# Mask products between the attention units of a two-block transformer kernel, and compressed-attention products at other steps

## The reference, cut to what matters

```
p_cmp = masked_softmax(q @ kc.T, valid_c)      # compressed keys: one per 16 tokens, 32 columns kept
o_cmp = p_cmp @ vc                             # kc, vc: a two-layer gelu MLP over blocks of 32 tokens
o_slc = masked_softmax(q @ ks.T, causal) @ vs  # all blocks are selected at 512 tokens
o_win = masked_softmax(q @ kw.T, causal) @ vw  # the window is 512 tokens
out   = g0 * o_cmp + g1 * o_slc + g2 * o_win
```

## Time and profile before

| | |
|---|---|
| median of 3 runs | 2499.64 us (2499.09 to 2499.95) |
| the profiled execution, its own time | 2497.28 us |
| its span, first to last instruction | 2495.5 us |
| mean granted TensorE clock | 0.964 |
| PE busy | 2416.5 us (97%) |
| DVE, ACT, POOL busy | 1514.0, 925.5, 843.5 us |
| attention loop, first score to last V product | about 175.1 to 385.6 us |

### The profile page before, as it was taken

One profiled execution on the slowest core, in us unless ns is written; L12 is line 12 of the kernel. 1 busy time (PEld: TensorE's weight loads), 2 busy tenths in 40 slices (PEclk: granted clock), 3 DMA queues, 4 the chain that ended last, 5 costly groups with the idle time before them and its releaser, 6 DMA issues.

```text
span 2495.5 us, 29550 instructions
## 1 busy us (share of the span) xinstructions
PE 2416.5 (97%) x11184; PEld 1990.0 (80%) x11184; DVE 1514.0 (61%) x2571; ACT 925.5 (37%) x1341; POOL 843.5 (34%) x620
## 2 busy tenths in 40 slices
PE   7999998999999999899999999999999999999996
PEld 6877767788888788778888888888888788888885
DVE  4364234777753476656797774553222588888887
ACT  4353232433333544543333233443222333333332
POOL 0030001112100000000007877886772576666652
PEclk9996579999999999999999999999999999999998
DMA  6211004488632222133346666557767799999994
GB/s 210 86 51 51 1 1 132 153 288 276 231 101 93 80 89 68 51 118 98 99 130 153 148 144 148 119 120 207 202 148 244 273 368 361 359 359 354 359 350 136
DMA packets 205115, 434.21 MB, mean 174 GB/s; under 512 B 54112, under 2 KB 104304, under 8 KB 204464
## 3 DMA queue, kind: packets, MB, share of 16 engines
q1 hardware_dynamic: 81840, 251.79, 29.6%
q0 software_dynamic: 72368, 119.73, 17.9%
q10 hardware_dynamic: 50768, 60.82, 7.1%
HBM read 369.22 MB, written 63.05 MB: 173 GB/s over the span
## 4 chain that ended last, share of the span: by engine, by line
PE 93%; DVE 3%; ACT 2%; DMA 1%; issue 1%; POOL 0%; DVEq 0%; SPq 0%; ACTq 0%
PE PS L272 27%; PE PS L273 27%; PE PS L274 26%; PE PS L1974 2%; PE PS L2048 2%; PE PS L2104 1%; PE PS L2204 1%; PE PS L2036 1%; PE PS L1976 1%; PE PS L2182 1%; PE PS L2006 1%; DMA RAW<-in_w_in 1%; ACT A L452 0%; DVE PS L1778 0%; PE PS L422 0%
## 5 line engine op out<-in xcount | busy, mean ns | idle before, releaser
L267 DVE TENSOR_TENSOR WL<-RAW,WH 128x1024 fp32r<-128x1024 f32 (+1 forms) x414 | 506.1, 1223 | 605.7 <-ACT WH L261 603.2
L272 PE MATMUL PS<-HH,WH 128*128 128x512 f32 x1696 | 669.4, 395 | 8.7 <-DVE HL L433 7.1
L273 PE MATMUL PS<-HL,WH 128*128 128x512 f32 x1696 | 661.5, 390 | 0.0
L274 PE MATMUL PS<-HH,WL 128*128 128x512 f32 x1696 | 661.4, 390 | 0.0
L830 POOL DMA_INDIRECT gates<-A,PLACE x256 | 438.4, 1712 | 333.8 <-DVE PLACE L1709 206.4
L261 ACT ACTIVATE WH<-RAW 128x1024 fp32r<-128x1024 f32 (+1 forms) x414 | 434.9, 1052 | 280.5 <-PE PS L274 254.5
L272 PEld LDWEIGHTS PS<-HH,WH 128*128 128x128 f32 x1696 | 319.4, 188 | 80.6 <-DVE HL L433 10.0
L274 PEld LDWEIGHTS PS<-HH,WL 128*128 128x128 f32 x1696 | 319.2, 188 | 66.8
L273 PEld LDWEIGHTS PS<-HL,WH 128*128 128x128 f32 x1696 | 319.6, 188 | 65.2 <-issue 1.0
L272 PE MATMUL PS<-WH,WGH 128*128 128x512 f32 x768 | 299.1, 389 | 4.7 <-DVE WGL L1762 4.0
L274 PE MATMUL PS<-WH,WGL 128*128 128x512 f32 x768 | 298.8, 389 | 0.0
(11 more groups left out here) (334 smaller groups left out, 2842.1 us busy)
## 6 DMA issues: line engine op xcount, KB each, us to landing
RAW<-in_peer_u SPq DMA_DIRECT2D x128, 512.0 KB, 3.6
RAW<-in_peer_v SPq DMA_DIRECT2D x128, 512.0 KB, 7.1
A<-in_w_ada POOLq DMA_DIRECT2D x48, 512.0 KB, 4.6
A<-gates ACTq DMA_DIRECT2D x32, 768.0 KB, 11.1
A<-acts ACTq DMA_DIRECT2D x32, 768.0 KB, 14.3
RAW<-in_ffn_up SPq DMA_DIRECT2D x44, 512.0 KB, 4.9
gates<-A POOLq DMA_DIRECT2D x16, 1024.0 KB, 6.6
acts<-GATE SPq DMA_DIRECT2D x64, 256.0 KB, 2.2
```

What stands on the lines that cost most here:

```text
L267: nc.vector.tensor_tensor(WLr[:, slot(c), 0:w], RAW[:, slot(c), 0:w], WH[:, slot(c), 0:w], ALU.subtract).then_inc(sem("low_done"), 1)
L272: nc.tensor.matmul(out, L[0], R[0], start=first, stop=False)
L273: nc.tensor.matmul(out, L[0], R[1], start=False, stop=False)
L274: return nc.tensor.matmul(out, L[1], R[0], start=False, stop=last)
```

## The change

`paced(bank, n)` is a new function on PE: n products of `MASKr[:, 0, :]` with the whole 256 columns of `MASKr`, type fp32r, written to a bank whose content is not needed. Nothing reads them. It is called with 28 at step 6 ahead of the wait for the gelu, with 5 in each of the 44 units ahead of the wait for its exponentials (the bank is the one which the unit's transposes then overwrite), and with 20 ahead of the barrier behind the loop. The compressed scores are issued 4 heads (8 instructions) at a step in eight steps, not 8 heads in four. The rest of the compressed branch follows later; its V products come at steps 32, 34, 36 and 41.

```diff
+        CS_AT = (12, 13, 14, 15, 17, 18, 19, 20)
+        CS_TAKEN_AT = (16, 21)
+        PTC_AT = (27, 29)
+        CO_AT = (32, 34, 36, 41)
 # ACT
-                if s == 19:
+                if s == 23:
                     act.wait_ge(sem("late_shifted"), 1)
-                if s in (24, 26):
-                    n = (s - 24) // 2
+                if s - 1 in PTC_AT:
+                    n = PTC_AT.index(s - 1)
 # DVE
-                if s in (14, 17):
-                    n = (s - 14) // 3
+                if s in CS_TAKEN_AT:
+                    n = CS_TAKEN_AT.index(s)
-                if s == 18:
+                if s == 22:
                     dve.wait_ge(sem("cs_taken"), 2)
-                if s == 20:
+                if s == 24:
-                if s == 21:
+                if s == 25:
-                if s == 22:
+                if s == 26:
-                if s in (28, 30, 32, 34):
-                    t = (s - 28) // 2
+                if s - 1 in CO_AT:
+                    t = CO_AT.index(s - 1)
 # PE
+            def paced(bank, n):
+
+                for _ in range(n):
+                    nc.tensor.matmul(PS[:, bank, 0:2 * P], MASKr[:, 0, :], MASKr.rearrange("p s n -> p (s n)"),
+                                     start=True, stop=True)
                 if s == 6:
+                    paced(3 + s % 2, 28)
                     pe.wait_ge(sem("root_gelu"), 2)
-                if s in (12, 13, 15, 16):
-                    t = (12, 13, 15, 16).index(s)
+                if s in CS_AT:
+                    t, half = CS_AT.index(s) // 2, CS_AT.index(s) % 2
                     pe.wait_ge(sem("mlp_kept"), 3)
                     if t == 2:
                         pe.wait_ge(sem("cs_taken"), 1)
-                    for h in range(NH):
+                    for h in range(4 * half, 4 * half + 4):
 ...
-                    last.then_inc(sem("cs_ready"), 1)
-                if s in (23, 25):
-                    n = (s - 23) // 2
+                    if half:
+                        last.then_inc(sem("cs_ready"), 1)
+                if s in PTC_AT:
+                    n = PTC_AT.index(s)
-                if s in (27, 29, 31, 33):
-                    t = (s - 27) // 2
+                if s in CO_AT:
+                    t = CO_AT.index(s)
                     wait(pe, "at_stored", u - 1)
+                    paced(3 + u % 2, 5)
                     pe.wait_ge(sem("at_exp"), u + 1)
+            paced(0, 20)
             barrier(pe, "attention")
```

## The result

| | before | changed |
|---|---|---|
| median | 2499.57 us (20 runs) | 2479.51 us (20 runs) |
| lowest to highest | 2487.5 to 2500.79 | 2460.04 to 2499.46 |
| ratio, 95% interval | | 0.9934 [0.9913, 0.9955] |
| the profiled execution: own time, span, clock | 2497.28, 2495.5, 0.964 | 2496.31, 2494.5, 0.976 |

The change is faster by 0.66%, some 16 to 20 us, less than half or just half of what was forecast (39.2 us). The fastest execution, 2460.04 us at a mean clock of 0.991, is at the forecast of 2460.4; most of the others lie in clusters near 2469, 2479 and 2496 us, at 0.987, 0.983 and 0.976. The ratio is one of means, without the changed kernel's two executions at 2499.5 us, which count as slow; the medians alone give 0.992. Time and clock of the 20 executions stand in one order: the lower the clock, the longer the run.

The account below looks back on a forecast made before the run. Loop bound by PE, mostly at 1.2 GHz; -57.1 - 4.6 - 2.4 + 26.4 - 1.5 = -39.2 us gives 2458.1 us profiled, 2460.4 median. Range 2454 to 2470, or 2452 to 2482 with A's near part.

Parts of the forecast that it names:

- a held clock: Attention loop: the filler keeps PE's clock up, giving the forecast median of 2460.4 us; chance 0.70.
- Rival A: Thin middle of the loop, steps 8 to 25: clock falls and is lifted again, 2470 to 2500, written 2485 us; chance 0.18.
- Part 1: Gelu's wait: 28 products at 0.12 us, 3.4 us, fit inside the 3.8 us wait and cost nothing.
- Part 2: Loop clock: if it stays up, 124.2 us become 67.1 (-57.1) and 9.9 us become 5.3 (-4.6).
- The price of the scores at full clock: Compressed scores, 0.222 us each at half clock: taken to scale by 0.54, to 0.12 us each at full clock.
- Part 3: Five products in each of 44 units: 220 x 0.12 us, all on PE's path, +26.4 us.
- Part 4: Compressed scores issued in halves: same instructions, no cost; 0.96 us of them a step at full clock.
- Part 5: Compressed V products moved apart: PE's wait for DVE's sum goes, -2.4 us; the moved softmax costs 0, at most 3 us.
- rival C: Softmax steps at full clock: PE runs into late ACT or DVE work, 2456 to 2466 us; chance 0.07.
- Part 6: Barrier behind the loop: 20 products are covered by the 3.3 us wait; the turn stays at full clock, -1.5 us.
- Rival B: Attention loop: filler neither holds nor lifts the clock and costs 0.21 us a product, 2544 us; chance 0.05.
- the sum without the turn's 1.5 us: Turn: by the skill page's rule that transposes do not count as busy, no gain there, total -37.7 us.

Follow-up runs that it names:

- e2: Changed kernel without the five products in each unit, keeping the 28 at the gelu's wait and the 20 at the barrier: median 2485.81 us, ratio 0.9952.
- e1: Changed kernel without any of the 268 filler products, only the moved compressed scores, softmax and V products: median 2494.06 us, ratio 1.0008.
- e4: Changed kernel with one head in four of the compressed scores computed, 48 of 64 products left out: median 2476.44 us, ratio 0.9902.
- g4: Changed kernel with one head in four of the compressed scores and 15 products, not 5, in steps 22 to 24: median 2459.77 us, ratio 0.9845.
- g2: Changed kernel with blocks of 10 products in the eight compressed-score steps and steps 22 to 27, none in other units: median 2455.93 us, ratio 0.9831.
- g1: Changed kernel with 15 products in one block, not 5, in steps 22, 23 and 24: median 2481.44 us, ratio 0.9921.
- g3: Changed kernel with 15 products, not 5, in the eight compressed-score steps alone: median 2489.01 us, ratio 0.9967.
- f2: Changed kernel with unit filler only at compressed-score steps, step 16 and steps 22 to 27, partly between scores, 115 products: median 2492.68 us, ratio 0.998.
- f4: Changed kernel again without any edit, as a control with a second profile: median 2479.83 us, ratio 0.9946.
- f1: Changed kernel with three of the five products moved between the heads' scores in the eight compressed-score steps: median 2508.75 us, ratio 1.0033.

## Why the prediction was wrong

The step that failed is the second, "if it stays up, 124.2 us become 67.1 (-57.1)", and with it the choice to give a held clock 0.70. Rival A, with 0.18, is what happened, at the place that it named (the compressed scores and the small products, "the one mix of work that no row shows at full clock") and with a median of 2479.5 where it had 2485. In the profiled execution 30.7 us, 40.4 us and about a quarter of 27.5 us were at half speed, 78 us. By the ratio 0.54 that is 36 us lost, and 2496.3 - 36 = 2460, where 2458.1 was forecast: all but 2 us of the error is there. The median lies inside the stated range of 2452 to 2482, but in the part that came from A and not from the forecast; its 19 us over 2460.4 are some 41 us at half speed by the same ratio, an estimate.

- Part 1, the gelu: right. 28 products from 208.69 to 212.18 us, 0.125 us each, and no wait left in the changed kernel's profile.
- Part 2: mis-sized. My argument was that every fall stood in an idle stretch. It was drawn from a kernel in which the first idle stretch had taken the clock down ahead of the thin steps, so that these could not show what they do to a clock that is up. e2 shows it: first block of scores, fall, 122 us at half. The other support, that units of 128 and 256 columns ran at 1.00 from 175 to 205.4 us, did not carry either: units of 128 columns are the four-head units, and the clock fell in them in nine of the twelve profiles of the table. A had named the scores and the small products, not these.
- The price of the scores at full clock: right. 0.126 us each against 0.222 at half, a ratio of 0.57.
- Part 3: 0.13 us a product, not 0.12; 28 us, not 26. At half speed it is 0.24 us (five in 1.18 us from 256.23 us on, in a step without scores), and in the profiled execution a good part was paid at that price.
- Part 4, "no cost": right as work, and the blocks of eight did not save the clock either.
- Part 5: the wait of 2.4 us is gone (right), no wait for DVE's softmax came (right; rival C is out). That it also took the V products away from the steps where they had lifted the clock I had not counted: they stood at step 27 and now begin at step 32, and in e1 the loop was at half until 375 us.
- Part 6, the turn: right, 5.14 to 3.71 us, -1.4.
- Rival B, the filler never holds nor lifts: out. It held in steps 6 to 13 and, ten a unit, almost throughout. Its price at half speed was low too, 0.21 us where 0.24 was measured.

On the two rules of the Trainium skill (TensorE: Matmul & The Clock Gate). That continuous work brings full clock (section Why this matters for your kernels): by the changed kernel too it does not hold, 40.4 us of unbroken work at 0.50; e4, g4 and g2 show that what PE works on matters as well. That transposes do not count as busy (Part 4: PE-mode transpose): 32 of them ran at 1.00 in the changed kernel's turn, as they had brought the clock up before, so the sum without the turn's 1.5 us was the wrong one.

What stays open: why one execution passes the scores and the next does not. The falls came at different steps of the same program, always at the same kinds of step; that the moment at which the step comes decides is my reading, and no run tested it. g1 and g3 had few executions and wide spreads, so how the two places share the loss is not settled; that they are together nearly all of it is (g4). In four profiles (e2, e4, f2, f4) the clock was also down for some 3 us near 180 us, in the four-head unit of step 0; what decides that I did not try. Whether g2 owes its time to the blocks, to their number or to the empty steps between is not separated either.

## What to carry to other kernels

A trace in which the clock is already down says nothing on what a step would do to a clock that is up; look for the thinnest block of instructions in the stretch and take its fall as the likely case until a row shows otherwise. Here filler against a falling clock did best in one block at the thin steps and nowhere else: it costs its full time wherever the engine is the bound, and five everywhere (220) gave 20 us where ten at 14 of 44 steps (140) gave 43. Look at the spread too: a change that shortens the best execution by 40 us and the median by 20 is half done.

## What the runs showed of the hardware that I had not expected

- The granted clock can be 0.50 for 122 us (e2) and 133 us (f1) with TensorE busy all the time, and 0.99 in the same kernel for 31 us of other units without any filler. What PE runs matters, not only whether it waits: every fall behind the gelu began at the compressed scores or the four-head units (table above).
- A change from 64-row float32 products to a 128-row fp32r product and back costs about 0.27 us at full clock (0.65 us against 0.38), more than the filler product itself (0.128 us).
- The same program without any change gave 2460 to 2499 us on one core, and the kernel before had executions near 2487.5 among its usual 2499.5, all by how long the clock was down.
